# The closing stage of a decoder step: two of five tiles' expert rows weighted on ScalarE and added on GpSimd

## What is computed

```
def hier_moe(h, p):
    ...
    w_assign = (jax.nn.softmax(top_v, axis=-1) * g_w[:, None]).reshape(-1)
    ...
    return jnp.zeros((n, D_MODEL), h.dtype).at[tok_s].add(out[dest] * w_s[:, None].astype(h.dtype))

def merge_and_ffn(x, ssm_out, attn_heads, g_mrg, p):
    ...
    return x + hier_moe(h, p).reshape(bsz, t, D_MODEL)

def rms_norm(x, g):
    y = xf * lax.rsqrt(jnp.mean(xf * xf, axis=-1, keepdims=True) + NORM_EPS)
    return (y * g.astype(jnp.float32)).astype(x.dtype)

    y_prompt = rms_norm(xp, g_final)
    y_sample = rms_norm(xs, g_final)
```

## Time and profile before

| | us |
|---|---|
| median of 3 runs | 1394.59 |
| lowest, highest of the runs | 1392.9, 1445.29 |
| profiled execution | 1392.34 |
| its span | 1390.7 |
| start of the phase combine in it (first issue) | 1359.58 |
| start of the last final scaling | 1386.09 |

### The profile page before, as it was taken

The page is one execution under the profiler, slowest core; times in us unless marked ns, Lnnn a source line. Parts: engine busy times, 40 slices in busy tenths (PEclk is TensorE's granted clock), DMA queues, the critical chain, the costliest instruction groups (busy, mean ns, idle before and its releaser), DMA issues. The chain is left out here.

```text
span 1390.7 us, 17123 instructions
## 1 busy us (share of the span) xinstructions
PE 1111.5 (80%) x6170; PEld 703.0 (51%) x6170; DVE 389.9 (28%) x961; ACT 270.3 (19%) x567; POOL 237.4 (17%) x604
## 2 busy tenths in 40 slices
PE   5999997877775877998999965987777777777760
PEld 5999997754344665666774533332222222322220
DVE  4447341657742333131232133000000000000005
ACT  6323222334431122112000110110010000101102
POOL 0008911188404120000000001011000000000010
PEclk9999997668877888557999975999999999999995
DMA  8321342220009530433006023999999999999946
GB/s 339 104 85 62 105 171 80 65 105 1 5 12 305 157 114 21 196 142 121 0 0 264 31 112 124 422 421 422 421 421 422 421 422 421 422 421 422 422 191 219
DMA packets 71241, 299.32 MB, mean 215 GB/s; under 512 B 12070, under 2 KB 30374, under 8 KB 44678
## 3 DMA queue, kind: packets, MB, share of 16 engines
q1 hardware_dynamic: 60734, 274.79, 49.8%
q0 software_dynamic: 9296, 22.71, 4.7%
q10 hardware_dynamic: 1152, 1.05, 0.2%
HBM read 284.27 MB, written 25.58 MB: 223 GB/s over the span
## 5 line engine op out<-in xcount | busy, mean ns | idle before, releaser
L1880 PE MATMUL ps<-arena 128*64 128x512 f32 x1024 | 242.4, 626 | 70.1 <-DMA arena<-in_w_exp 52.3
L346 PE MATMUL ps<-local_project 128*128 128x288 f32 (+4 forms) x1608 | 205.2, 290 | 17.2 <-DVE local_project L485 16.4
L346 PEld LDWEIGHTS ps<-local_project 128*128 128x128 f32 (+1 forms) x1608 | 204.2, 184 | 17.7 <-DVE local_project L485 16.4
L1880 PEld LDWEIGHTS ps<-arena 128*64 128x64 f32 x1024 | 79.4, 143 | 222.3 <-issue 200.2
L1880 PE MATMUL ps<-local_late,arena 128*64 128x512 f32 x512 | 117.7, 603 | 32.6 <-DMA local_late<-in_w_exp 31.3
L1928 DVE SCALAR_TENSOR_TENSOR arena<-arena,ps 128x512 f32<-128x512 f32 x16 | 11.0, 688 | 310.9 <-ACT arena L1912 310.9
L1880 PEld LDWEIGHTS ps<-local_late,arena 128*64 128x64 f32 x512 | 40.2, 138 | 109.2 <-issue 109.2
L1536 PE MATMUL ps<-arena 128*128 128x512 f32 (+1 forms) x160 | 71.3, 606 | 1.4 <-DVE arena L1656 1.4
L1850 POOL TENSOR_TENSOR arena<-arena 1x1 f32<-1x1 f32 x16 | 2.9, 184 | 348.8 <-ACT arena L1920 348.8
L1904 ACT ACTIVATE arena<-ps 128x512 f32<-128x512 f32 x34 | 18.5, 594 | 217.3 <-PE ps L1863 217.3
L1931 DVE SCALAR_TENSOR_TENSOR arena<-arena,ps 128x512 f32<-128x512 f32 x16 | 11.0, 688 | 159.5 <-PE ps L1880 159.5
(11 more groups left out here) (381 smaller groups left out, 1521.0 us busy)
## 6 DMA issues: line engine op xcount, KB each, us to landing
arena<-in_w_exp SPq DMA_DIRECT2D x128, 1024.0 KB, 25.5
local_late<-in_w_exp SPq DMA_DIRECT2D x64, 1024.0 KB, 25.8
arena<-in_w_rest SPq DMA_DIRECT2D x9, 1024.0 KB, 5.7
arena<-in_w_wide SPq DMA_DIRECT2D x6, 1040.0 KB, 4.9
scratch_sig<-arena POOLq DMA_DIRECT2D x16, 288.0 KB, 2.6
arena<-scratch_sig SPq DMA_DIRECT2D x1, 4608.0 KB
arena<-in_x SPq DMA_DIRECT2D x2, 2048.0 KB, 7.9
arena<-in_cache POOLq DMA_DIRECT2D x32, 128.0 KB, 3.7
```

What stands on the lines that cost most here:

```text
L346: mm = pe.matmul(out, stationary(s, k), moving(m, k), start=k == 0 and a == 0, stop=k == KD - 1 and a == 2)
L1880: mm = pe.matmul(c.ps[SLOTS * q:SLOTS * (q + 1), bank, :], tokens[:, k0 + k, SLOTS * q:SLOTS * (q + 1)], raw[p][q][:, k], start=first and ...
```

## The change

For tiles 1 and 3, ScalarE multiplies the returned rows in place by their weight (an activation Copy with the weight as scale), and GpSimd adds the two products to x, one after the other. VectorE keeps the adds of tiles 0, 2 and 4 in the old form, and all norms. The semaphore that says that a tile's sum is done is split in two, one counted by VectorE and one by GpSimd; a new one counts weighted halves. On VectorE, `add_rows(2)` now stands ahead of tile 0's norm and `add_rows(4)` ahead of tile 2's. On ScalarE, the weighting of tile 1 stands ahead of tile 0's Square and that of tile 3 ahead of tile 2's Square. SyncE's code is the same.

```
         @block.scalar
         def _(act):
+            def scale_rows(i):
+                for j in range(2):
+                    act.wait_ge(r_in[i][j], 16)
+                    act.activation(R[0:ROWS[i], i, j], R[0:ROWS[i], i, j], ACT.Copy, scale=c.wt[0:ROWS[i], j, i:i + 1]).then_inc(row_scaled, 1)
+
             for i in range(TILES):
                 r = ROWS[i]
-                act.wait_ge(x_done, i + 1)
+                if i % 2 == 0 and i + 1 < TILES:
+                    scale_rows(i + 1)
+                act.wait_ge(x_done[i % 2], i // 2 + 1)
                 act.activation(y[0:r, i], c.x2[0:r, i], ACT.Square, accum_out=ss[0:r, i:i + 1]).then_inc(sq_done, 1)
                 act.wait_ge(mean_ready, i + 1)
                 act.activation(ss[0:r, i:i + 1], ss[0:r, i:i + 1], ACT.Sqrt).then_inc(root_done, 1)
+
+        @block.gpsimd
+        def _(pool):
+            link = c.gsteps.on(pool)
+            for i in range(1, TILES, 2):
+                x = c.x2[0:ROWS[i], i]
+                for j in range(2):
+                    pool.wait_ge(row_scaled, i + j)
+                    ins = pool.tensor_tensor(x, R[0:ROWS[i], i, j], x, ALU.add)
+                    if j == 0:
+                        link(ins)
+                ins.then_inc(x_done[1], 1)
...
-                ins.then_inc(x_done, 1)
+                ins.then_inc(x_done[0], 1)
...
-                if i + 1 < TILES:
-                    add_rows(i + 1)
+                if i % 2 == 0 and i + 2 < TILES:
+                    add_rows(i + 2)
```

More of the change, by code:

```diff
@@ L1945, in combine @@
         g_in, r_in, x_done, sq_done, y_done, stored = (
-            sem("g_final_in"), [[sem(f"r_in{i}{j}") for j in range(2)] for i in range(TILES)], sem("c_x_done"),
+            sem("g_final_in"), [[sem(f"r_in{i}{j}") for j in range(2)] for i in range(TILES)], [sem("x_done_by_vector"), sem("x_done_by_gpsimd")],
             sem("c_sq_done"), sem("c_y_done"), sem("c_stored"))
-        mean_ready, root_done = sem("c_mean_ready"), sem("c_root_done")
+        mean_ready, root_done, row_scaled = sem("c_mean_ready"), sem("c_root_done"), sem("row_scaled")
         block = ctx.enter_context(nc.Block())
```

## The result

The change takes 1398.07 us in the median of 20 runs, the kernel before 1395.57 in the median of 20; the ratio is 1.003 with a 95% interval of 1.0019 to 1.0041, so 2.6 to 5.7 us slower: clear of zero, and far below 2%. (Medians of both include a few long runs; the ratio leaves disturbed ones out.) The profiled execution took 1397.01 us with a span of 1395.3, against 1392.34 and 1390.7.

The account below looks back on a forecast made before the run. VectorE and, at the start, transfers were taken to set the 31.2 us closing phase. +5.5 and -0.75 gave +4.8 us: 1397.1 from the profile, 1399.4 from the median, middle 1398.5 us; range 1392.5 to 1404.5.

Parts of the forecast that it names:

- First stretch: Closing phase up to tile 0's mean, which comes after tile 2's adds: 1376.2 instead of 1370.7, +5.5 us.
- exclusion: Closing phase: while VectorE or GpSimd works on two SBUF operands, the other doesn't; total +4.8 us, chance 0.77.
- rival A: Closing-phase adds: no exclusion, VectorE and GpSimd run freely; -0.9 us, 1392.8; chance 0.10.
- Second stretch: Closing phase from tile 0's mean to the last final scaling: 14.65 us instead of 15.40, -0.75 us.
- turns: Closing-phase adds alternate: GpSimd's ends 2.28 us after VectorE's, VectorE's 1.15 us after GpSimd's.
- B: GpSimd's four closing-phase adds are dearer, 3.7 us each: +10 us in all, 1403.7; chance 0.10.
- C: GpSimd's own price is 2.79 us for 256 columns, 11.2 us per closing-phase add: +40 us, 1434; chance 0.01.
- the base of 1393.7: Whole-kernel time taken for no change, the footing on which the forecast and the rivals were counted.

Follow-up runs that it names:

- experiment 1: Kernel before plus nine sections behind its end, VectorE and GpSimd alone or together; four two-operand VectorE instructions took 4.87 us alone, 13.24 beside GpSimd adds.
- experiment 2: Kernel before plus four GpSimd adds on spare rows that nobody waits for; last final scaling +7.30 us, ratio to before 1.0064.
- experiment 7: The change with x of tiles 0, 2 and 4 copied into PSUM by TensorE; last final scaling -0.91 us against before, ratio to before 0.9999.
- experiment 9: Kernel before, tile i's mean between tile i+1's adds, tile 3 weighted by ScalarE and summed by TensorE in PSUM, its norm last; ratio to before 0.9976.

## Why the prediction was right

Its bound and its direction: VectorE's row of two-operand work sets the phase, GpSimd can't overlap with it, and the 5.1 us taken off VectorE come back as waits. Experiments 1, 2 and 7 show this in three separate ways.

By its terms. First stretch, to tile 0's mean: +5.5 forecast; measured 1376.33 - 1359.81 = 16.52 against 1370.69 - 1359.58 = 11.11, **+5.41**. Not all of that is exclusion: in experiment 7, without it, tile 0's mean still comes 2.25 us late, because it stands behind tile 2's rows (rival A had 2.7). There the second stretch is 3.16 us shorter than before, which more than makes up for it. Second stretch, to the last scaling: -0.75 forecast; measured 14.42 against 15.40, **-0.98**. The small difference is in the turns: from the end of tile 1's scaling (1380.03) to the end of tile 4's adds (1386.60) four turns took 6.57 us, and I had 2.28 + 1.15 + 2.28 + 1.15 = 6.86. A pair of turns took 3.3 us in experiment 1 too, for my 3.43; the column price, extended from short rows, was a little high (2.34 us alone for my 2.42), and the rest is in the gap between two ends, read from one row of 256 columns. Sum +4.8 forecast, +4.43 measured; the timed ratio gives +4.2.

The price of a GpSimd add, extended from 64 and 256 columns to 1024, was 2.42 us; the first one took 2.36. The mechanisms B and C (3.7 and 11.2 us) are out with that. The single instructions came as foretold: GpSimd's first pair 2.36 and 3.20 us (2.4 and 3.4 forecast), VectorE's adds of tile 2 2.14 and 3.24 (2.1 and 3.5), those of tile 4 3.37 and 3.24 (3.5 each). Rival A named the right alternative world, and experiment 7 entered it.

The time in us fits better than it deserves. I forecast 1398.5 and the median is 1398.07, but the base of 1393.7 (its middle worked out 0.2 too high) was 1.9 below the median of 20 runs of the kernel before, 1395.57, and the two medians differ by 2.5 us, not by 4.8: two errors that cancel. The range, 1392.5 to 1404.5, also holds no change and rival A, so the time alone would not have told exclusion from free overlap; the stretched instructions do.

Of the two statements of the Trainium skill, the wider one held: GPSIMD Engine Reference, section 8 (Key points), names VectorE instructions with two SBUF inputs among those that contend, and the trace agrees (13.24 us for 4.87). The other statement of the Trainium skill, Advanced Engine Details and Errata, section Mode Summary, names 2-port instructions only; by it the adds of the change would have been free, and experiment 1's first row says they were not.

What I had too narrow was the other side: I expected exclusion only where GpSimd reads two operands. A copy takes its turn too (8.01 us for 4.87).

## What to carry to other kernels

Before work is moved from VectorE to GpSimd, ask what VectorE does at that time: if its long instructions read two SBUF tensors, or are of the one-operand form of experiment 1, the two engines share one row of work and most of GpSimd's price is simply added (four adds that nobody waits for cost 7.3 of their 9.2 us). With one of VectorE's operands in PSUM the loss is gone, but no run here was timed faster by using GpSimd; whether it pays where VectorE is idle was not tried. Here ScalarE and TensorE were the better places to move work to (experiment 9). And when a stall can be moved by reordering but the end stays, suspect a shared resource before you look for a better order.

## What the runs showed of the hardware beyond what was expected

- A GpSimd copy of 128x1024 float32 takes 0.99 us and a GpSimd add 2.3; beside VectorE's two-operand instructions (1.22 us each) the pairs take 2.0 and 3.3 us.
- VectorE's one-operand multiply-add with constants, float32, takes 0.63 us alone, about half of the two-operand form, and 2.8 us beside a GpSimd add: of the pairs tried, this form is stretched by the largest factor.
- With work pending on both, the engines took strict turns: in the first mixed section of experiment 1 four pairs took 13.24 us, 3.3 each, and neither engine got two instructions in a row: VectorE's took 3.40, 3.36, 3.36 and 3.36 us, GpSimd's 2.34 and then 3.32, 3.32 and 3.31.
